# Neighbourhood attention in query tiles of 16 columns by 8 rows, with 256 keys in place of 512 and values rearranged by tile

## The reference, cut to what matters

```
s_win = jnp.einsum('brchd,brjwhd->bhrcjw', qg, k_blk).astype(jnp.float32) * scale
c = jnp.arange(GRID_W)
col_start = jnp.clip(c - NA_WIN_W // 2, 0, GRID_W - NA_WIN_W)
in_win = (c[None, :] >= col_start[:, None]) & (c[None, :] < col_start[:, None] + NA_WIN_W)
...
s_win = jnp.where(in_win[:, None, :], s_win + bias[None], -1e30)
s_meta = jnp.einsum('brchd,bmhd->bhrcm', qg, km).astype(jnp.float32) * scale
s = jnp.concatenate([s_win.reshape(B, H, rows, GRID_W, kh * GRID_W), s_meta], axis=-1)
p = jax.nn.softmax(s, axis=-1).astype(v.dtype)
```

## Time and profile before

| what | before |
|---|---|
| median of 3 runs | 2146.49 us (2143.98 to 2146.57) |
| the profiled execution's own time | 2147.23 us |
| its span on the core | 2145.3 us |
| PE busy | 2084.6 us, 97% |
| DVE busy | 1370.0 us, 64% |
| ACT busy | 921.1 us, 43% |
| POOL busy | 284.9 us, 13% |
| DMA read from HBM | 177.68 MB, 84 GB/s over the span |

### The profile page before, as it was taken

The page is one execution under the profiler, slowest core; times in us unless marked ns, Lnnn a source line. Parts: engine busy times, 40 slices in busy tenths (PEclk is TensorE's granted clock), DMA queues, the critical chain, the costliest instruction groups (busy, mean ns, idle before and its releaser), DMA issues.

```text
span 2145.3 us, 27154 instructions
## 1 busy us (share of the span) xinstructions
PE 2084.6 (97%) x10757; PEld 1659.7 (77%) x10757; DVE 1370.0 (64%) x2004; ACT 921.1 (43%) x1494; POOL 284.9 (13%) x336
## 2 busy tenths in 40 slices
PE   8998999999999999999999999999999999999998
PEld 7765568888888777688888888666878768888887
DVE  5889745967934488668678363565655435768753
ACT  4245545454443345444544442243423224544542
POOL 3420100000000243100000012010445220000000
PEclk9999999999999999999999999999999999999999
DMA  8530112224232432132332323121121323323231
GB/s 210 144 80 24 25 59 99 82 95 137 79 98 82 118 89 84 45 117 80 108 118 79 109 89 114 57 76 40 59 60 40 99 72 97 115 100 98 100 102 73
DMA packets 167336, 190.71 MB, mean 89 GB/s; under 512 B 21669, under 2 KB 125402, under 8 KB 167210
## 3 DMA queue, kind: packets, MB, share of 16 engines
q1 hardware_dynamic: 160592, 173.93, 25.8%
q0 software_dynamic: 6288, 14.93, 2.8%
q10 hardware_dynamic: 330, 0.12, 0.0%
HBM read 177.68 MB, written 2.17 MB: 84 GB/s over the span
## 4 chain that ended last, share of the span: by engine, by line
PE 82%; DVE 11%; ACT 3%; issue 2%; DMA 1%; ACTq 0%; POOL 0%; POOLq 0%; DVEq 0%
PE banks L457 70%; PE banks L2861 3%; DVE wl L392 2%; ACT wh L388 1%; PE banks L2980 1%; DVE sm L1546 1%; DVE big L1589 1%; PE banks L1600 1%; DMA big<-even_cmp_w 1%; PE banks L1636 1%; DVE t L1156 1%; PE banks L1382 1%; DVE big L1159 1%; PE banks L2551 1%; PE banks L2630 1%
## 5 line engine op out<-in xcount | busy, mean ns | idle before, releaser
L457 PE MATMUL banks<-uTh,wh 128*128 128x512 f32 (+1 forms) x1424 | 550.2, 386 | 5.5 <-DVE uTl L648 1.7
L457 PE MATMUL banks<-uTh,wl 128*128 128x512 f32 (+1 forms) x1424 | 539.0, 379 | 0.0
L457 PE MATMUL banks<-uTl,wh 128*128 128x512 f32 (+1 forms) x1424 | 538.7, 378 | 0.0
L457 PE MATMUL banks<-wh,hTr 128*128 128x512 f32 x1552 | 488.3, 392 | 0.3 <-DVE hTr L2169 0.3
L392 DVE TENSOR_TENSOR wl<-stg,wh 128x2048 fp32r<-128x2048 f32 x133 | 311.1, 2339 | 214.9 <-ACT wh L388 214.3
L457 PEld LDWEIGHTS banks<-wh,hTr 128*128 128x128 f32 x1552 | 292.1, 188 | 64.4 <-DVE wl L392 2.5
L388 ACT ACTIVATE wh<-stg 128x2048 fp32r<-128x2048 f32 x133 | 253.0, 1902 | 191.6 <-PE banks L457 172.5
L457 PEld LDWEIGHTS banks<-uTh,wh 128*128 128x128 f32 x1424 | 268.9, 189 | 56.2 <-issue 3.6
L457 PEld LDWEIGHTS banks<-uTh,wl 128*128 128x128 f32 x1424 | 268.6, 189 | 51.0
L457 PEld LDWEIGHTS banks<-uTl,wh 128*128 128x128 f32 x1424 | 269.0, 189 | 47.3 <-issue 0.5
L457 PE MATMUL banks<-wl,hTr 128*128 128x512 f32 x776 | 302.6, 390 | 0.0
(11 more groups left out here) (370 smaller groups left out, 2800.1 us busy)
## 6 DMA issues: line engine op xcount, KB each, us to landing
stg<-mlp_w_up SPq DMA_DIRECT2D x32, 1024.0 KB, 5.3
stg<-mlp_w_down SPq DMA_DIRECT2D x26, 1024.0 KB, 5.1
stg<-w_in SPq DMA_DIRECT2D x20, 1024.0 KB, 5.2
stg<-w_up SPq DMA_DIRECT2D x16, 1024.0 KB, 5.3
stg<-w_down SPq DMA_DIRECT2D x13, 1024.0 KB, 5.1
stg<-odd_w_in SPq DMA_DIRECT2D x16, 512.0 KB, 4.9
t<-p POOLq DMA_DIRECT2D x124, 64.0 KB, 2.1
big<-mlp_w_down SPq DMA_DIRECT2D x6, 1024.0 KB, 7.3
```

The source lines that it names most:

```text
L457: t = pe.matmul(outp, x, y, start=(start and k == 0 and m == 0), stop=(stop and k == n - 1 and m == 2))
```

## The change: what it does

A tile of 128 queries is now 16 columns by 8 rows of the grid, in place of two full rows. The four tiles need the key columns 0 to 31, 8 to 39, 24 to 55 and 32 to 63 (`WIN_AT`), so a block has 256 keys. They are worked in the order 0, 3, 1, 2 (`WIN_ORDER`). Queries are stored in tile order by `dve_nq` and `act_nq`, and the outputs put back by `act_na_out`. Keys stay where they are and are read with a stride (`window`). Values are needed as weights with keys on the partitions, so POOL writes `nv` to DRAM in 4 DMAs and reads each tile's 256 rows back in 2 (`pool_windows`, 8 in all), tiles 0 and 3 over the old `nv`. Tables are now three per head (the left edge, the middle, the right edge) of 8 rows by 32 columns: POOL fetches 8 rows by 48 columns in 8 DMAs to `bias48`, a place that all heads share, and makes the three by three additions. On DVE the call of `split_jobs` moves from the end of step n to behind `dve_na_max` of step n+1. The third place for a block's probabilities, `na_third`, moves into `p`.

```diff
-    c["c_win"] = np.tile(np.where(inw, 0.0, NEG).astype(np.float32)[::-1], (2, 1))
+    c["c_win"] = np.concatenate([np.tile(np.where(inw[16 * b:16 * b + 16, s0:s0 + 32], 0.0, NEG).astype(np.float32)[::-1], (8, 1))
+                                 for b, s0 in ((0, 0), (1, 8), (3, 32))], axis=1)
...
-        na_third = region(NVM_AT + 2 * T, [128, 2, T + META])
+        WIN_AT, WIN_KIND, WIN_ORDER = (0, 8, 24, 32), (0, 1, 1, 2), (0, 3, 1, 2)
+        WK = 256
+        nvw = [region(NVM_AT + (2 + c) * T, [128, T]) for c in range(2)] + [TT[2][:, 0:T], TT[3][:, 0:T]]
+        NV_TILES = [(0, 0), (0, 1), (3, 0), (3, 1)]
...
+        nvd = nc.dram_tensor("nvd", (T, T), F32, kind="Internal").ap()
+
+        def tiled(x):
+            return x.rearrange("p (b r c) -> p b r c", b=4, c=16)
+
+        def from_grid(x):
+            return x.rearrange("p (r b c) -> p b r c", b=4, c=16)
+
+        def window(x, b, r0=0, rows=8):
+            return x.rearrange("p (r c) -> p r c", c=64)[:, r0:r0 + rows, WIN_AT[b]:WIN_AT[b] + 32]
+
+        def values_at(b, ch):
+            return nv[:, NV_TILES.index((b, ch)), :] if b in (0, 3) else nvw[2 * (b - 1) + ch]
+
+        def values_dram(b, ch):
+            return bass.AP(nvd.tensor, (ch * 4 * 64 + WIN_AT[b]) * T, [[64 * T, 4], [T, 32], [1, T]])
...
-        NB = [nbr[:, 0, :], nbr[:, 1, :], Q[1][:, 0:896], big[:, at:at + 896]]
+        NB = [x[:, 0:768].rearrange("p (z a b) -> p z a b", z=3, b=32) for x in (nbr[:, 0, :], nbr[:, 1, :], Q[1], big[:, at:at + 896])]
+        bias48 = PF[:, 1632:2016].rearrange("p (a b) -> p a b", b=48)
...
-            for e2 in range(2):
-                src = bass.AP(pad.tensor, hh * 15 * 128 + e2 * 128, [[1, 64], [128, 14], [1, 64]])
-                pool.dma_start(b[e2 * 64:(e2 + 1) * 64, :].rearrange("p (a b) -> p a b", b=64), src).then_inc(
-                    *bias_in[hh % 2].next(("bias", hh)))
+            if hh:
+                pool.wait_ge(*g_misc.at(("bias", hh - 1)))
+            for e in range(8):
+                src = bass.AP(pad.tensor, hh * 15 * 128 + e * 128 + 32, [[1, 16], [128, 8], [1, 48]])
+                pool.dma_start(bias48[e * 16:(e + 1) * 16], src).then_inc(*bias_in[hh % 2].next(*([("bias", hh)] if e == 7 else [])))
             if hh == 0:
                 pool.wait_ge(*win_in.at("win"))
             pool.wait_ge(*bias_in[hh % 2].at(("bias", hh)))
-            bv = b.rearrange("p (a b) -> p a b", b=64)
-            pool.tensor_tensor(bv, bv, winm.unsqueeze(1).to_broadcast([128, 14, 64]), ALU.add).then_inc(
-                *g_misc.next(("bias", hh)))
+            for z, o in enumerate((16, 8, 0)):
+                t = pool.tensor_tensor(b[:, z], bias48[:, :, o:o + 32], winm[:, z * 32:z * 32 + 32].unsqueeze(1).to_broadcast(
+                    [128, 8, 32]), ALU.add)
+            t.then_inc(*g_misc.next(("bias", hh)))
...
+
+        def pool_windows(pool):
+
+            for i in range(NT):
+                pool.wait_ge(*kept(i, "nv"))
+                pool.dma_start(nvd[i * 128:(i + 1) * 128, :], nv[:, i, :]).then_inc(*nv_out.next(*(["nv"] if i == 3 else [])))
+            pool.wait_ge(*nv_out.at("nv"))
+            for x, b in enumerate(WIN_ORDER):
+                for ch in range(2):
+                    pool.dma_start(values_at(b, ch), values_dram(b, ch)).then_inc(*nv_in[x].next(*(["nv"] if ch else [])))
...
-        NP = [PP[:, 0:2, :], PP[:, 2:4, :], na_third]
+        NP = [PF[:, x * 2 * (WK + META):(x + 1) * 2 * (WK + META)].rearrange("p (g n) -> p g n", g=2) for x in range(3)]
...
-            return TP[:, 2 * (n % 2):2 * (n % 2) + 2, 0:T]
+            return TT[n % 2][:, 0:2 * WK].rearrange("p (g n) -> p g n", g=2)
...
+            i = WIN_ORDER[i]
             qv = [nq[g * 64:(g + 1) * 64, f, T - (i + 1) * 128:T - i * 128] for g in range(2)]
             for g in range(2):
-                pe.matmul(bank[g], qv[g], nk[g * 64:(g + 1) * 64, f, 0:T], start=True, stop=True)
+                pe.matmul(bank[g][:, 0:WK], qv[g], window(nk[g * 64:(g + 1) * 64, f, 0:T], i), start=True, stop=True)
...
-            o = (6 - 2 * i) * 64
+            z = WIN_KIND[WIN_ORDER[i]]
...
             for g in range(2):
-                dve.tensor_tensor(q[:, g, 0:T], bank[g], NB[(2 * f + g) % 4][:, o:o + T], ALU.add)
-            dve.tensor_copy(q[:, :, T:T + META], NA_META.rearrange("p (g n) -> p g n", g=2)).then_inc(
+                dve.tensor_tensor(q[:, g, 0:WK].rearrange("p (a b) -> p a b", b=32), bank[g][:, 0:WK].rearrange(
+                    "p (a b) -> p a b", b=32), NB[(2 * f + g) % 4][:, z], ALU.add)
+            dve.tensor_copy(q[:, :, WK:WK + META], NA_META.rearrange("p (g n) -> p g n", g=2)).then_inc(
                 *v_max.next(("na", n, "s")))
...
             for g in range(2):
-                for k in range(4):
+                for k in range(2):
                     s = slice(k * 128, (k + 1) * 128)
                     pe.transpose(bank[3 + g][:, s], q[:, g, s], ident)
...
-            act.activation(na_turned(n), banks[:, 3:5, :], ACT.Copy).then_inc(*a_flip.next(("na", n)))
+            act.activation(na_turned(n), banks[:, 3:5, 0:WK], ACT.Copy).then_inc(*a_flip.next(("na", n)))
...
+            i = WIN_ORDER[i]
+            if f == 0:
+                pe.wait_ge(*nv_in[n].at("nv"))
...
-            for k in range(4):
+            for k in range(2):
                 for g in range(2):
                     hh = 2 * f + g
-                    pe.matmul(o[g], nv[:, k, hh * 64:hh * 64 + 64], na_turned(n)[:, g, k * 128:(k + 1) * 128],
+                    pe.matmul(o[g], values_at(i, k)[:, hh * 64:hh * 64 + 64], na_turned(n)[:, g, k * 128:(k + 1) * 128],
...
-                act.activation(onT[:, f, :], bank[5][:, ::-1], ACT.Copy).then_inc(*a_keep.next(("on", f)))
+                act.activation(from_grid(onT[:, f, :]), tiled(bank[5][:, ::-1]), ACT.Copy).then_inc(*a_keep.next(("on", f)))
...
                     dve_na_prob(dve, n - 2)
                 if 0 <= n - 1 < N:
                     dve_na_max(dve, n - 1)
+                if n:
+                    split_jobs("dve", n)
                 for jb in jobs_done(n):
                     dve_job(dve, jb)
                 if 0 <= n - 2 < N:
...
                 if n == 0:
                     split_jobs("dve", 0)
-                split_jobs("dve", n + 1)
...
             for hh in range(8):
                 pool_bias(pool, hh)
+                if hh == 1:
+                    pool_windows(pool)
```

More of the change, by code:

```diff
@@ L164, in build @@
         m8 = sb("m8", [128, 3, 8])
-        winm = sb("k_c_win", [128, 64])
+        winm = sb("k_c_win", [128, 96])
         lb = sb("lb", [128, 2, 2, 4])
@@ L208, in build @@
         bias_in = [signal(f"bias_in{i}", 16) for i in range(2)]
+        nv_out, nv_in = signal("nv_out", 16), [signal(f"nv_in{x}", 16) for x in range(4)]
         stored = signal("stored", 16)
@@ L2342, in dve_nq @@
                 dve.wait_ge(*p_mm.at(("nq", f)))
-                dve.tensor_scalar(nq[:, f, :], bank[NQ_BANKS[f]][:, ::-1], 0.125, None, ALU.mult).then_inc(*v_keep.next(("nq", f)))
+                dve.tensor_scalar(tiled(nq[:, f, :]), from_grid(bank[NQ_BANKS[f]][:, ::-1]), 0.125, None, ALU.mult).then_inc(*v_keep.next(("nq", f)))
                 yield
@@ L2349, in act_nq @@
                 act.wait_ge(*p_mm.at(("nq", f)))
-                act.activation(nq[:, f, :], bank[NQ_BANKS[f]][:, ::-1], ACT.Copy, scale=0.125).then_inc(*a_keep.next(("nq", f)))
+                act.activation(tiled(nq[:, f, :]), from_grid(bank[NQ_BANKS[f]][:, ::-1]), ACT.Copy, scale=0.125).then_inc(*a_keep.next(("nq", f)))
                 yield
@@ L2604, in pe_na_flip @@
             for g in range(2):
-                t = pe.transpose(NA_META_T[:, g * 128:(g + 1) * 128], q[:, g, T:T + META], ident)
+                t = pe.transpose(NA_META_T[:, g * 128:(g + 1) * 128], q[:, g, WK:WK + META], ident)
             t.then_inc(*p_flip.next(("na", n)))
```

## The result

The change runs at 2121.77 us (median of 4, 2120.69 to 2122.69) against 2146.02 for the kernel before beside it: ratio 0.9885, 95% interval 0.9873 to 0.9898, some 24 us less. The profiled execution took 2120.69, its span is 2118.9; before it was 2147.23 and 2145.3. So by the profiles 26.4 us went.

The account below looks back on a forecast made before the run. TensorE was taken as the bound, though not without gaps: 23.2 us from its list plus 9.0 of waits and clock less 0.5 for POOL beside VectorE gave 31.7, from 2146.49 to 2114.8, range 2110 to 2127.

Parts of the forecast that it names:

- TensorE's list: Attention on TensorE: shorter scores (6.9), half the transposes (8.2) and fewer output product records (8.2) save 23.2 us.
- that rival: Scores on TensorE: strided keys are read no faster, so 6.9 us stay away, 2122; chance 0.07.
- The wait at the meta scores: TensorE waiting for VectorE's copy of a block's meta part, less covered by shorter scores: zero taken, at most 6.9 us.
- Steps 9 and 12, 3.1 + 2.7 + 0.8: Moved subtraction in attention: step 9's wait goes (3.1 us) and its slow clock (2.7); step 12's wait shrinks by 0.8.
- Step 6: TensorE in attention waits for ScalarE's copy of a job, behind its rounding: 1.7 us in place of 2.0.
- Step 2 and the end: Attention: TensorE's 1.65 us wait for VectorE's job copy goes; at the end ScalarE copies half, saving 0.4.
- Values through memory, zero: Writing `nv` to DRAM and reading it back before the first output product: about ten microseconds to spare, cost zero.
- The tables: POOL making tables 2 to 7 during attention: 8.2 us each, ready before they are needed, cost zero.
- the third rival: Tables 2 and 3 late behind 2 MB of reads in POOL's queue: table 3 6 us late, 2124; chance 0.12.
- Serial pieces: POOL's table pieces land one after another: 18.7 us a table, three long waits, 2155; chance 0.04.
- POOL beside VectorE, 0.5: POOL's 18 additions in the attention holding up VectorE's instructions: 0.5 us lost, at the other end 11.
- The waits stay in another place: Meta scores wait for the subtraction now ahead of the meta copy: 9.0 us of waits and clock return, 2123; chance 0.12.

Follow-up runs that it names:

- The run with the later half job: The change, with ScalarE's job copy ahead of its second weight rounding in step 6 and a half job moved from step 6 to 7 on TensorE: 2122.60 us, ratio 0.9894.
- the two runs on the order: Kernel before with only VectorE's subtraction moved behind division and maximum: ratio 0.9979; the change with that subtraction put back to the end of the step before: ratio 0.9923.
- the four executions of the old order: Profiled executions of the kernel before: unchanged, with 60, 1 and 4 added POOL DMAs; attention stretch 145.3, 145.2, 145.1 and, in the fourth (4 DMAs), 140.7 us.
- the run with the copy first: The change, with ScalarE's copy of a job in step 6 put ahead of its second rounding of weights: 2119.37 us, ratio 0.9876.
- the eight programs of the table above: Kernel before; it with 4, 60 small or one spreading POOL DMA added; the change; it without value moves, with 20 more DMAs, with one DMA a table: drains 2.07 to 10.81 us.
- the run with the order alone: Kernel before with only VectorE's subtraction of weights moved behind the division and maximum of a step: ratio 0.9979, attention stretch 136.4 us.

## Why the prediction was right, and where it was not

The forecast was 2114.8 (2110 to 2127), faster; the result is 2121.77, 7.0 above it. For the profiled execution it was 2115.5 against 2120.69: 5.2 too low. Only these 5.2 can be taken apart by the traces. Two of the signs that were named for a wrong forecast came: VectorE's maximum waited for POOL at block 4, and the granted clock fell behind step 6 (0.66 over 5 us).

- *TensorE's list, 23.2.* Mis-sized. The scores came out at 0.63 with strided keys, as taken; that rival is out. But halving the records did not halve the time: eight output records take 0.59 and sixteen 1.02, four transposes 0.59 and eight 1.02. By these two pairs a group has some 0.16 of its own that does not shrink. (Where a half job stands directly ahead of the transposes, they take 0.87 and 0.44 in the chain, and save the same 0.43.) 1.29 saved a block in place of 1.45: 20.6.
- *The wait at the meta scores*, taken as zero: right, no such row. The run with the later half job shows what it is worth when uncovered, 2.95.
- *Steps 9 and 12, 3.1 + 2.7 + 0.8.* Right in mechanism, by the two runs on the order. From the start of block 8 to that of block 10 the profiles differ by 6.5 beyond the shorter blocks, and by 1.9 over steps 12 and 13, where 0.8 was taken: nothing is late next there. But the 3.1 + 2.7 was the price where the division is held: 1.9 of it was that, and the clock came only with it, in three of the four executions of the old order. In the fourth, from block 8 to block 10, only 1.9 is left of the 6.5.
- *Step 6*, the wait forecast at 1.7: 1.59 came. What was missed is the slow clock behind it, 1.8, which the 2.0 of before had not brought. My text put slow clock only where it had been. From the score of block 5 to that of block 6 the change is 0.3 slower than before where the shorter block alone would save 1.3: a loss of 1.6 where a gain of 0.3 was in the sum.
- *Step 2 and the end*, 1.65 and 0.4: right (no wait in step 2; at the end 1.11 became 0.69).
- *Values through memory, zero*: right, by the run without them. The first output product came at 1374.2 (forecast 1373.6).
- *The tables*: 8.2 each was right where nothing else moves (7.8: eight issues 4.2, landing 1.5, additions 2.1). But table 3 came at 1387.7, not 1376.5, past its due time of 1384.5. What I had left out of the sum, and kept for the third rival, happened: table 2's pieces stood behind the 2 MB of reads. In the run without the moves they land 1.59 behind the last issue, here 13.11.

```profile
1360.16 4.27 POOL L2477 DMA_DIRECT2D p<-pad  x8
1377.54 2.14 POOL L2482 TENSOR_TENSOR q<-p,k_c_win 128x256 f32<-128x256 f32 x3 [13.11 <-DMA p<-pad]
...
1385.59 2.13 POOL L2482 TENSOR_TENSOR big<-p,k_c_win 128x256 f32<-128x256 f32 x3 [1.45 <-DMA p<-pad]
1387.81 0.42 DVE L2602 TENSOR_TENSOR p<-banks,q 128x256 f32<-128x256 f32 x1 [2.39 <-issue]
```

  VectorE waited 2.39 for it (the last row, its first addition of block 4; the profile names nobody that it waited for, but it starts as POOL's additions end). TensorE did not: it was in a half job, with an output product and the transposes still ahead of what needed that block's scores taken away. The rival's lateness was there and its price was not. Serial pieces are out (landing 1.5 behind the last of eight issues).
- *POOL beside VectorE, 0.5.* No loss of TensorE's time can be named in the change. The contention is there, and mostly on the other side: POOL's three additions take 2.13, but beside VectorE's subtraction

```profile
1394.20 5.01 POOL L2482 TENSOR_TENSOR big<-p,k_c_win 128x256 f32<-128x256 f32 x3 [1.61 <-DMA p<-pad]
...
1395.59 2.34 DVE L394 TENSOR_TENSOR wl<-stg,wh 128x2048 fp32r<-128x2048 f32 x1 [0.40 <-ACT wh L390]
```

  5.01, while the subtraction took 2.34 in place of 2.29 (2.88 in the run with the copy first). The Trainium skill (GPSIMD Engine Reference, Key points) says that POOL contends with VectorE's instructions that read two inputs from SBUF; this pair agrees, which no row read before had shown, with nearly all of the loss on POOL.
- *The end of the program* was not in the sum at all: 3.0 for POOL's drain. The forecast's sentence that POOL is done before the next stage was true of its work, and left out what its DMAs cost at the close of the program.
- *The waits stay in another place*, the first rival (2123): its number came closer than the forecast's, its mechanism did not. Steps 9, 12 and 15 have no wait. Alone in its case the forecast reached only to 2119. The 2121.77 lies in the range because rivals had widened it, and none of their prices was paid: that is in part luck.

So of the 5.2 by which the profiled execution came later: 2.6 is the list, 3.0 the drain, 0.8 scatter ahead of the attention; the waits and clock gave 9.6 (30.2 - 20.6), about 1 more than the forecast's 8.5. The 9.6 is against an execution of before with the held division; against the other (140.7) it would be 5.0.

## What to carry to other kernels

Halving the instructions of a short group on TensorE does not halve its time; read the price of the new count from a group of that count. When work on one engine is reordered, list for each step what then stands ahead of the instruction that TensorE asks for next: the same two subtractions were nearly free in one step (a wait of 0.68) and brought one of 2.95 with the half job beside them moved. Take a wait's price from more than one execution where the old code allows it: here one trace in four had 4.6 us less of it. Count the DMAs that are issued from POOL too, and look at what the queues do behind the last result: the best cover inside the program does not hide it.

## What the runs showed of the hardware that was not expected

- POOL's closing drain: 2.07 to 10.81 us over the eight programs of the table above, in steps of 81.7 ns, the size of one DMA's, not always rising with their number. SP closes 4.7 us after its start, so it ends the program when it is longer than that.
- The slow clock moves about between executions of the same code. The first score, with unchanged code ahead of it, came between 1358.3 and 1361.5 in the profiles; in that part the run with the order alone has five microseconds at 0.66 from 125 and at 0.72 from 1325, where the profiles of before and of the change have 1.00. A single profile can't tell 2 us of gain from this. Nor does the length of a wait settle it: behind the 1.59 of step 6 the clock fell in all five profiles that have this wait, behind the 1.65 of step 2 in none.
- POOL's addition held VectorE's division for 1.6 to 1.9 us in four traces of five, whether it started up to 0.26 before it or up to 0.42 behind its start; in the fifth, at 0.44, the division took its 0.90 and the addition 2.40 in place of 2.1.
